# A new front half for a one-core decoder step: head in parts, rotation in place, four heads per score product, another job order

## The chip, the cores and the metric

One core of one Trainium2 chip runs the kernel. The metric is the device time of one execution in microseconds; lower is better.

## The reference, cut to what matters

One decoder layer over 256 prompt rows and 8 decode rows (264 columns in all, kept as features x rows), D = 1024, float32:

```
h = RMSNorm(x); proj = h @ w_in            # columns: pool u (512) | q (512) | k (512) | v (512)
mixer A: windows 2,4,8,16: trailing mean of u minus u, per-group map w_pool, scale s_pool
mixer B: attention, 8 heads x 64, rotary q and k; prompt rows causal over 256 keys,
         each decode row over its 256 paged keys (cache_k, cache_v) and its own key
x = x + concat(A, B) @ w_out
x = x + cross attention(RMSNorm(x)), 4 heads x 256, over 256 memory rows:
        prompt: mem_k, mem_v = RMSNorm(mem) @ w_ck, @ w_cv;  decode rows: cached memory keys and values
x = x + relu(RMSNorm(x) @ w_up)^2 @ w_down;  y = RMSNorm(x)
```

The outputs are y, the rotated k, v, the last rows of u, and the memory keys and values.

## The kernel before, in words

All weights stream through TensorE in 120 chunks of 256 rows x 512 columns (512 KB each). The groups stand in a fixed order: `in` 1 (q), `in` 2 (k), `in` 3 (v), `in` 0 (u), `ck`, `cv`, `out`, `cq`, `co` (chunks 0 to 55), then `up` and `down` (56 to 119). A product has to keep float32 precision with float32r operands, so each operand is split into a high part (ScalarE, line 881, `split_hi`, `w_hi<-raw`) and a low part (VectorE, line 1080, `split_lo`, `w_lo<-raw,w_hi`), and every tile is multiplied in three passes (high x high, high x low, low x high): 24 products of 264 columns a chunk at line 865. `raw` has 3 slots, `w_hi` and `w_lo` 4; a chunk is split three chunks ahead (`SPLITS_AT`), when the chunk four before it has been used.

The norm's factor is applied behind the product. ScalarE squares the tiles of x (`square`), GpSimd adds the squares (line 1306, `add_squares`), one product with ones sums over partitions (line 686, job `("stat", ...)`), ScalarE takes the root, VectorE the reciprocal (`rstd`).

The rest of the work is a list of jobs, each in a slot behind one chunk (`plan_jobs`); every engine walks through chunks and jobs in this one order. `S` h is the scores of prompt head h (lines 697 and 698, 64 rows of the array each, two products), followed on VectorE and ScalarE by mask, maximum, exponential and scaling; `P_T` transposes the probabilities (line 708), `O` multiplies by the values (lines 718, 719). `cS` b, `cP_T` b, `cO` b, `c_attn` b do the same for four decode rows each (b = 0, 1), on four column groups of 32 (helper `tile4`, line 666), with the products for the own key at lines 737 and 743; `c_attn` gathers the rows (line 753). `m_tile` k rounds a tile of the memory rows into `act_hi`/`act_lo`; `differences` and `pool` are mixer A; `xP_*` is the cross attention of the prompt, `xS`, `xc_T`, `xc_O`, `xc_attn` that of the decode rows (line 813 gathers).

The rotation of q and k (`take_out`, groups 1 and 2): ScalarE copies four quarters of a tile from PSUM with halves swapped (`swapped`), VectorE multiplies the tile by the cosines (line 1126), GpSimd the swapped one by the sines (line 1318), VectorE adds (line 1130). Group `in` 1 is in PSUM until `rstd` is there.

SyncE issues all loads in order: for each chunk first the units planned before it (`LOADS_AT`: pages of the caches `K`, `V`, memory rows `m`, memory keys `mK` and values `mV`, 512 KB each), then the weights (line 624). Four banks of PSUM belong to a running group; jobs take the bank that was used longest ago of the others.

Of the kernel before, what the change touches and what calls it, by code (L numbers as in the profile page):

```python
# [34 lines left out]
P = 128  # L35
# [24 lines left out]

CK = 2
# [3 lines left out]
AHEAD = SPLIT - 1  # L65
STAGE = 6
# [3 lines left out]
SOFTS = 3  # L70
SOFT_TS = 5
# [69 lines left out]
def plan_jobs():  # L141

    slots = {c: [] for c in range(-1, NC)}

    def put(c, *names):
        slots[c].extend(names)

    put(2, ("stat", "x"))
    k_end, v_end, u_end = last_chunk("in", 2), last_chunk("in", 3), last_chunk("in", 0)  # L160
# [3 lines left out]
    put(v_end + 1, ("v_nat", 0), ("v_nat", 1), ("v_nat", 2), ("cP_T", 0), ("m_tile", 0), ("m_tile", 1))  # L164
    put(v_end + 2, ("P_T", 2), ("P_T", 3), ("O", 0), ("m_tile", 2), ("m_tile", 3))
    put(v_end + 3, ("S", 4), ("S", 5), ("m_tile", 4), ("m_tile", 5))
    put(u_end, ("cO", 0), ("cS", 1), ("O", 1), ("m_tile", 6), ("m_tile", 7))
    put(u_end + 1, ("P_T", 4), ("P_T", 5), ("c_attn", 0))
    put(u_end + 2, ("cP_T", 1), ("S", 6), ("S", 7))
    put(u_end + 3, ("O", 2), ("stat", "m"), ("stat_col", "m"))  # L170
    put(u_end + 4, ("differences",))
    put(u_end + 5, ("P_T", 6), ("P_T", 7))
    put(u_end + 6, ("cO", 1), ("O", 3), ("pool", 0), ("pool", 1))
    put(u_end + 7, ("pool", 2), ("pool", 3), ("c_attn", 1))
    put(last_chunk("out", 1) + 3, ("stat", "c"))
    a, b = last_chunk("cq", 0), last_chunk("cq", 1)
# [12 lines left out]
ORDER = [j for c in range(-1, NC) for j in JOBS[c]]  # L189


def plan_banks():

    jobs, groups, uses, stamp, now = {}, {}, [0] * 8, [-1] * 8, 0
    hold_from, hold_to = ORDER.index(("xS", 0, 0)), ORDER.index(("xS", 1, 1))

    def take(bank):
        nonlocal now  # L200
        now += 1
        uses[bank] += 1
        stamp[bank] = now
        return uses[bank] - 1

    for c, (g, w, n, k, last) in enumerate(CHUNKS):
        if k == 0:
            for bank in banks_of(g):
                groups[g, bank] = take(bank)
        for j in JOBS[c]:  # L210
            if j[0] in ("m_tile", "differences"):
                continue
            if j[0] == "xS" and j != ("xS", 0, 0):
                jobs[j] = jobs["xS", 0, 0]
                continue
            taken = set(banks_of(g)) if not last else set() if (w, n) == ("cq", 1) or g + 1 == len(GROUPS) else set(banks_of(g + 1))
            if hold_from - 2 <= ORDER.index(j) <= hold_to:
                taken.add(7)
# [34 lines left out]


def plan_loads(kinds):

# [1133 lines left out]
```

## Time and profile before

| | us |
|---|---|
| median of 3 runs (lowest to highest) | 449.91 (447.57 to 452.04) |
| profiled execution: span from first to last instruction | 447.9 |
| TensorE busy | 423.8 |
| VectorE busy | 266.7 |
| ScalarE busy | 229.5 |
| GpSimd busy | 39.1 |
| moved by DMA | 96.8 MB, mean 216 GB/s |

The profile is of one execution, and its busy times are sums over its span of 447.9 us; its own time with what lies around the span is not recorded, so the span stands beside the median of the runs, 449.91. Matmuls are pipelined, so the distance between starts of two records says what one costs. A float32 product (no r) leaves two records.

### The profile page before, as it was taken

What the parts mean: (1) busy time and instruction counts of PE and PEld (TensorE: products, weight loads), DVE (VectorE), ACT (ScalarE), POOL (GpSimd) and SP (SyncE); (2) the same over time, 40 slices, a digit from 0 to 9 for tenths busy, and PEclk for the clock granted to TensorE, in tenths of its full rate; (3) what the DMA queues carried; (4) which work ended last, traced back from release to release, by engine and by line L of the source; (5) the groups of instructions that cost most, each with busy time, mean ns of one, the idle gap of its engine ahead of it and who ended that gap; (6) DMA issues with size and microseconds to landing.
All of it is one profiled execution on the core that took longest, in us unless ns stands there. A gap on an engine that the chain in (4) does not pass through costs nothing.

```text
span 447.9 us, 8424 instructions
## 1 busy us (share of the span) xinstructions
PE 423.8 (95%) x3346; PEld 393.0 (88%) x3346; DVE 266.7 (60%) x417; ACT 229.5 (51%) x411; POOL 39.1 (9%) x49
## 2 busy tenths in 40 slices
PE   2699899999999999999999999999999999999992
PEld 2699787787988999795599999999999999999992
DVE  2676787889454587654316967766666633444304
ACT  5777657664355474434026746656666533353202
POOL 0621001450000030000002200000000000020000
PEclk9979999999999999999989999999999999999998
DMA  7899897485699887597716655555555555545002
GB/s 273 286 280 343 324 265 240 161 283 170 185 352 317 334 277 284 173 368 281 266 36 246 235 190 187 189 190 189 187 187 184 186 180 176 176 168 179 1 1 97
DMA packets 42409, 96.80 MB, mean 216 GB/s; under 512 B 3954, under 2 KB 20466, under 8 KB 42234
## 3 DMA queue, kind: packets, MB, share of 16 engines
q1 hardware_dynamic: 40962, 93.03, 60.9%
q10 hardware_dynamic: 1408, 3.23, 1.9%
q8 instruction: 27, 0.44, 0.4%
q14 instruction: 12, 0.10, 0.1%
HBM read 91.94 MB, written 4.54 MB: 215 GB/s over the span
## 4 chain that ended last, share of the span: by engine, by line
PE 77%; ACT 8%; DVE 7%; issue 3%; DMA 2%; POOL 2%; ACTq 0%; SPq 0%; DVEq 0%; POOLq 0%
PE psum L865 68%; PE psum L666 4%; ACT w_hi L881 2%; DVE w_lo L1080 2%; DMA raw<-in_w_in 2%; POOL ssq L1306 1%; ACT swapped L881 1%; PE psum L791 1%; PE psum L778 1%; ACT soft L1024 1%; ACT act_hi L881 1%; DVE soft L1191 1%; PE psum L813 1%; DVE stats L1194 1%; PE psum L686 0%
## 5 line engine op out<-in xcount | busy, mean ns | idle before, releaser
L1080 DVE TENSOR_TENSOR w_lo<-raw,w_hi 128x1024 fp32r<-128x1024 f32 x82 | 103.1, 1268 | 90.5 <-ACT w_hi L881 90.0
L865 PE MATMUL psum<-act_hi,w_hi 128*128 128x264 f32 (+1 forms) x416 | 122.5, 294 | 9.0 <-DVE act_lo L1084 8.0
L881 ACT ACTIVATE w_hi<-raw 128x1024 fp32r<-128x1024 f32 x82 | 85.5, 1054 | 76.3 <-PE psum L865 64.2
L865 PE MATMUL psum<-act_lo,w_hi 128*128 128x264 f32 (+1 forms) x416 | 119.7, 288 | 0.0
L865 PE MATMUL psum<-act_hi,w_lo 128*128 128x264 f32 (+1 forms) x416 | 119.5, 287 | 0.0
L865 PEld LDWEIGHTS psum<-act_hi,w_hi 128*128 128x128 f32 x416 | 80.2, 193 | 12.9 <-DVE w_lo L1080 8.3
L865 PEld LDWEIGHTS psum<-act_lo,w_hi 128*128 128x128 f32 x416 | 80.0, 192 | 0.2
L865 PEld LDWEIGHTS psum<-act_hi,w_lo 128*128 128x128 f32 x416 | 79.8, 192 | 0.0
L1306 POOL TENSOR_TENSOR ssq<-ssq,sq 128x264 f32<-128x264 f32 (+1 forms) x31 | 25.4, 818 | 339.5 <-ACT sq L902 337.0
L865 PE MATMUL psum<-hid_hi,w_hi 128*128 128x264 f32 x176 | 50.1, 284 | 0.0
L865 PE MATMUL psum<-hid_lo,w_hi 128*128 128x264 f32 x176 | 50.1, 284 | 0.0
L865 PE MATMUL psum<-hid_hi,w_lo 128*128 128x264 f32 x176 | 50.0, 284 | 0.0
L865 PE MATMUL psum<-mix_hi,w_hi 128*128 128x264 f32 x128 | 37.2, 291 | 0.7 <-DVE mix_lo L1256 0.7
L865 PE MATMUL psum<-mix_hi,w_lo 128*128 128x264 f32 x128 | 37.2, 290 | 0.0
L865 PE MATMUL psum<-mix_lo,w_hi 128*128 128x264 f32 x128 | 37.1, 290 | 0.0
L865 PEld LDWEIGHTS psum<-hid_hi,w_hi 128*128 128x128 f32 x176 | 33.2, 189 | 0.0
L865 PEld LDWEIGHTS psum<-hid_lo,w_hi 128*128 128x128 f32 x176 | 33.1, 188 | 0.0
L865 PEld LDWEIGHTS psum<-hid_hi,w_lo 128*128 128x128 f32 x176 | 33.1, 188 | 0.0
L1080 DVE TENSOR_TENSOR w_lo<-raw_more,w_hi 128x1024 fp32r<-128x1024 f32 x16 | 19.5, 1231 | 15.3 <-ACT w_hi L881 15.3
L952 ACT ACTIVATE hid<-hid 128x264 f32<-128x264 f32 x32 | 13.3, 416 | 27.6 <-DVE hid L1146 27.6
L865 PE MATMUL psum<-act_lo,w_hi_more 128*128 128x264 f32 x96 | 27.3, 285 | 0.0
L865 PE MATMUL psum<-act_hi,w_hi_more 128*128 128x264 f32 x96 | 27.3, 284 | 0.0
(155 smaller groups left out, 769.1 us busy)
## 6 DMA issues: line engine op xcount, KB each, us to landing
raw<-in_w_down SPq DMA_DIRECT2D x20, 512.0 KB, 3.3
raw<-in_w_up SPq DMA_DIRECT2D x18, 512.0 KB, 4.3
raw<-in_w_in SPq DMA_DIRECT2D x16, 512.0 KB, 5.4
raw_more<-in_w_up SPq DMA_DIRECT2D x14, 512.0 KB, 4.4
raw_more<-in_w_down SPq DMA_DIRECT2D x12, 512.0 KB, 4.2
keysT<-in_cache_k SPq DMA_DIRECT2D x16, 256.0 KB, 4.4
stage<-in_cache_v SPq DMA_DIRECT2D x16, 256.0 KB, 4.1
raw<-in_w_ck SPq DMA_DIRECT2D x8, 512.0 KB, 5.2
```

What stands on the lines that cost most here:

```text
L666: return pe.matmul(out, lhsT, rhs, start=start, stop=stop, skip_group_check=True, tile_position=(0, 32 * j))
L778: last = pe.matmul(B[:, qt * MEM:(qt + 1) * MEM], q2T[:, 2 * h + d, qt * P:(qt + 1) * P], mkT[:, 2 * h + d, :], start=d == 0, stop=d == 1)
L791: last = pe.matmul(B[:, d * SEQ:(d + 1) * SEQ], mv[:, c, h * MHD + d * P:h * MHD + (d + 1) * P], pT[:, c * SEQ:(c + 1) * SEQ], start=c == ...
L813: last = pe.matmul(B[:, 4 * (AT * half + f):4 * (AT * half + f) + 4], opart[:, OPART["xc_O", b, half] % 2, f * P:(f + 1) * P], con("rowsel ...
L865: mm = pe.matmul(out, a, b, start=first and m == 0, stop=end_ and m == 2)
L881: return nc.scalar.activation(out, in_, ACT.Copy, scale=scale)
L952: nc.scalar.activation(hid[:, 1, j % 2, :], hid[:, 0, j % 2, :], ACT.Square).then_inc(square_ready, 1)
L1024: last = nc.scalar.activation(dst, src, ACT.Exp, bias=stats[:, slot, x:x + 1], accum_out=stats[:, slot, 2 + x:3 + x])
L1080: V.tensor_tensor(lo_of(c), raw_of(c), hi_of(c).bitcast(F32), ALU.subtract).then_inc(w_lo_ready, 1)
L1191: V.tensor_tensor(soft[:, slot, 0:3 * P], B[:, 0:3 * P], causal, ALU.add).then_inc(bank_free[PLACE[job][0]], 1)
L1194: V.tensor_reduce(stats[:, slot, 1:2], soft[:, slot, P:3 * P], AX_X, ALU.max, negate=True).then_inc(max_ready, 1)
L1306: nc.gpsimd.tensor_tensor(ssq[:, m % 2, 0:n], ssq[:, m % 2, 0:n], sq[:, k % SQ_SLOTS, 0:n], ALU.add).then_inc(sq_added, 1)
```

## The change

It leaves the weight products, their number and the second half (`up`, `down`) as they are, and rebuilds what stands before. In parts:

- **Head in parts.** The first weight tile is loaded, split and multiplied in two halves (`open_first_group`: pass by pass over four banks, not bank by bank). Gains and the first x tiles are issued by ScalarE. 16 products of zeros (`WARM`) run on TensorE first. `("stat", "x")` moves from slot 2 to slot 3.
- **Rotation in place.** The columns of `w_in` and of the key cache are ordered so that the two halves of a head lie in different tiles (`TURNED`). ScalarE copies each tile once to `qT` or `kT` and frees the bank; GpSimd makes two products with the sines a pair (`crossed`); VectorE turns the pair in place in the new jobs `("turn", 0)` (slot 4, with the tables) and `("turn", 1)` (slot 7).
- **Four heads per score product.** A head now has 32 rows in each of two tiles. `scores(four)` issues 16 products on four row groups of 32, into four banks. The softmax works on four heads (`exp` h on ScalarE, `norm` four on VectorE).
- **Decode rows of both halves in one bank.** `cS` 0 and 1 add up into one bank, with one softmax, one `cP_T`, one own-key product, one `c_attn`; the probabilities are spread with zeros (`own_q`, `rows_of`). For the cross attention `xS`, `xc_T`, `xc_O`, `xc_attn` go by half of the heads, with 8 rows at once.
- **Memory rows in the mixer's operand tiles.** `act_*` and `mix_*` change roles, so `m_tile` need not wait for the products of `in` 0.
- **New job order and loads.** Slots and `LOADS_AT` are written out; banks, those of the groups too, go to the one used longest ago.
- `pool_differences` works on four windows at once where it can.

```diff
-    put(2, ("stat", "x"))
-    put(k_end + 2, ("S", 0), ("S", 1))
-    put(k_end + 3, ("cS", 0))
-    put(v_end, ("P_T", 0), ("P_T", 1), ("S", 2), ("S", 3))
...
-    put(a + 1, ("xP_S", 0), ("xP_S", 1), ("xS", 0, 0))
-    put(a + 2, ("xS", 0, 1))
-    put(a + 3, ("xP_T", 0), ("xP_T", 1))
...
+    put(3, ("stat", "x"))
+    put(4, ("turn", 0))
+    put(7, ("turn", 1), ("m_tile", 0))
+    put(8, ("m_tile", 1))
+    put(9, ("k_out",), ("S", 0), ("S", 1), ("S", 2), ("S", 3), ("m_tile", 2))
+    put(10, ("exp", 0), ("exp", 1))
+    put(11, ("exp", 2), ("qblock",), ("exp", 3), ("norm", 0))
+    put(12, ("m_tile", 3))
+    put(14, ("P_T", 0), ("m_tile", 4), ("P_T", 1), ("P_T", 2), ("v_nat", 0))
+    put(15, ("m_tile", 5), ("P_T", 3), ("S", 4), ("S", 5), ("S", 6), ("S", 7), ("m_tile", 6), ("m_tile", 7), ("cS", 0))
+    put(17, ("exp", 4), ("stat", "m"), ("stat_col", "m"))
+    put(18, ("exp", 5))
+    put(19, ("exp", 6), ("differences",))
+    put(20, ("v_nat", 1), ("exp", 7))
+    put(21, ("v_nat", 2), ("norm", 1))
+    put(22, ("cS", 1))
+    put(23, ("O", 0), ("P_T", 4))
+    put(24, ("cP_T",), ("O", 1))
+    put(25, ("P_T", 5))
+    put(26, ("cO", 0))
+    put(27, ("P_T", 6))
+    put(28, ("pool", 0), ("P_T", 7))
+    put(29, ("pool", 1), ("cO", 1), ("pool", 2))
+    put(30, ("pool", 3), ("O", 2), ("O", 3))
+    put(32, ("c_attn",))
+    put(41, ("stat", "c"))
+    put(45, ("xS", 0, 0), ("xS", 0, 1), ("xP_S", 0), ("xP_S", 1), ("xc_T", 0))
+    put(46, ("xP_T", 0), ("xP_T", 1))
+    put(47, ("xc_O", 0, 0), ("xP_O", 0), ("xP_S", 2), ("xS", 1, 0), ("xS", 1, 1), ("xc_O", 0, 1), ("xP_O", 1), ("xc_attn", 0), ("xP_S", 3), ("xc_T", 1))
+    put(48, ("xP_T", 2), ("xc_O", 1, 0), ("xc_O", 1, 1), ("xP_T", 3))
+    put(49, ("xP_O", 2), ("xc_attn", 1), ("xP_O", 3))
...
+LOADS_AT = {
+    10: [("m", 0)],
+    14: [("m", 1)],
+    15: [("K", 0)],
...
+    22: [("K", 7), ("V", 0)],
+    23: [("K", 6), ("V", 1)],
+    24: [("K", 5), ("V", 2)],
+    25: [("K", 4), ("V", 3)],
...
+    52: [("mK", 1, 0), ("mK", 1, 1), ("mK", 1, 2), ("mK", 1, 3), ("mK", 1, 4), ("mK", 1, 5), ("mK", 1, 6), ("mK", 1, 7)],
+    54: [("mV", 1, 0, 2), ("mV", 1, 0, 3), ("mV", 0, 1, 0), ("mV", 0, 1, 1), ("mV", 0, 1, 2), ("mV", 0, 1, 3), ("mV", 1, 1, 0), ("mV", 1, 1, 1), ("mV", 1, 1, 2), ("mV", 1, 1, 3)],
+}
...
+            def scores(four):
+
+                if four == 0:
+                    pe.wait_ge(rope_done, PAIRS)
+                for j in range(4):
+                    begin(("S", 4 * four + j))
+                for out, queries, keys in ((0, 0, P), (P, P, SEQ)):
+                    for half in range(2):
+                        for j in range(4):
+                            r, f = 32 * j, 2 * four + half
...
+            def warm_up():
+
+                pe.wait_ge(warm_ready, 1)
+                for _ in range(WARM):
+                    pe.matmul(psum[:, 7, 0:P], std[:, 0:P], std[:, 0:P], start=True, stop=True)
...
+            def turn(g):
+
+                scale = HD ** -0.5 if g == group["in", 1] else 1.0
+                for i in range(2 * g, 2 * g + 2):
+                    x = 2 * (i % 2)
+                    pair = (qT if g == group["in", 1] else kT)[:, x:x + 2, :]
+                    dve.wait_ge(crossed_ready, i + 1)
+                    then(V.scalar_tensor_tensor(out=pair, in0=pair, scalar=scale, in1=turned[:, 0, :].unsqueeze(1).broadcast_to([P, 2, T]),
+                                                op0=ALU.mult, op1=ALU.mult))
```

## Rows read from the trace of the kernel before

**Rows 1.** The page: busy time by engine, and the chain's shares.
```profile
PE 423.8 (95%) x3346; PEld 393.0 (88%) x3346; DVE 266.7 (60%) x417; ACT 229.5 (51%) x411; POOL 39.1 (9%) x49
...
PE 77%; ACT 8%; DVE 7%; issue 3%; DMA 2%; POOL 2%; ACTq 0%; SPq 0%; DVEq 0%; POOLq 0%
```

**Rows 2.** Waits of TensorE: us in total, times, longest.
```profile
PE psum L865 <- DVE act_lo L1084: 8.0, 1, 8.0
PE psum L686 <- POOL ssq L1306: 4.1, 1, 4.1
PE psum L697 <- DVE kT L1130: 1.4, 1, 1.4
PE psum L865 <- DVE mix_lo L1256: 0.7, 1, 0.7
```

**Rows 3.** The chain that ended last: start, us, what.
```profile
259.90 177.84 PE psum L865 x1464
```

**Rows 4.** Timeline of TensorE, 8 to 23 us: start, duration, line.
```profile
8.03 0.56 PE L865 MATMUL psum<-act_hi,w_hi 128*128 128x264 f32 x1 [8.03 <-DVE act_lo L1084]
...
18.01 0.29 PE L865 MATMUL psum<-act_hi,w_lo 128*128 128x264 f32 x1
22.39 1.22 PE L686 MATMUL psum<-ssq,const 128*128 128x264 f32 x2 [4.10 <-POOL ssq L1306]
```

**Rows 5.** Chain and timeline of the first 23 us: transfers, ScalarE, GpSimd, SyncE.
```profile
3.08 7.71 DMA raw<-in_w_in
...
8.87 1.06 ACT L881 ACTIVATE w_hi<-raw 128x1024 fp32r<-128x1024 f32 x1 [2.31 <-DMA raw<-in_w_in]
...
17.85 2.04 SPq L601 DMA_DIRECT2D keysT<-in_cache_k  x2
...
18.05 4.19 POOL L1306 TENSOR_TENSOR ssq<-ssq,sq 128x264 f32<-128x264 f32 x4
```

**Rows 6.** Groups of instructions, 0 to 60 us: count, busy us, mean ns, idle before.
```profile
L881 ACT ACTIVATE swapped<-psum 32x264 f32<-32x264 f32 x32 | 12.2, 382 | 1.3 <-PE psum L865 0.8
...
L1318 POOL TENSOR_TENSOR rope_b<-swapped,turned 128x264 f32<-128x264 f32 x8 | 6.1, 768 | 18.3 <-ACT swapped L881 13.4 <-DVE turned L1121 4.9
```

**Rows 7.** Timeline of TensorE at its jobs, and one from the chain.
```profile
47.42 0.50 PE L697 MATMUL psum<-kT,qT 64*128 64x128 f32 x4 [1.35 <-DVE kT L1130]
47.71 0.64 PE L698 MATMUL psum<-kT,qT 64*128 64x256 f32 x4
...
57.04 0.48 PE L697 MATMUL psum<-kT,qT 64*128 64x128 f32 x2
57.37 0.59 PE L698 MATMUL psum<-kT,qT 64*128 64x256 f32 x2
...
76.13 1.12 PE L743 MATMUL psum<-v_nat,ownp 8*128 8x512 f32 x2
...
86.14 0.95 PE L753 MATMUL psum<-const,opart 128*128 128x4 f32 x8
...
89.88 0.38 PE L735 MATMUL psum<-const,soft 128*128 128x128 f32 x2
...
179.14 3.45 PE psum L778 x16
...
182.52 1.94 PE L666 MATMUL psum<-keysT,qblock 128*32 128x256 f32 x32
...
222.91 1.95 PE L813 MATMUL psum<-const,opart 128*128 128x4 f32 x16
```

**Rows 8.** Windows: us, busy time by engine, granted clock, DMA share, GB/s.
```profile
24.00:28.00 4.00, 4.00 (x20) 4.00 (x19) 3.40 (x6) 3.07 (x9) 0.75 (x1) 0.50 0.87 254
...
84.00:224.00 140.00, 139.10 (x1052) 117.24 (x1052) 86.69 (x152) 64.22 (x116) 14.07 (x13) 1.00 0.77 268
...
188.00:200.00 12.00, 12.00 (x102) 10.80 (x95) 5.38 (x8) 4.57 (x7) 0.00 (x0) 1.00 1.04 350
...
224.00:228.00 4.00, 3.29 (x20) 3.23 (x20) 0.19 (x1) 0.20 (x1) 0.00 (x0) 0.74 0.00 0
```

More of the change, by code:

```diff
@@ L58 @@
 NKEY = PAST + 1
+PAIRS = AT
 CK = 2
@@ L167, in plan_jobs @@
[L167 to L175, printed above, removed]
@@ L189 @@
 ORDER = [j for c in range(-1, NC) for j in JOBS[c]]
+CHUNK_OF = {j: c for c in JOBS for j in JOBS[c]}
+CLOSER = {("cS", 0): ("cS", 1), ("cO", 0): ("cO", 1)}
+CLOSER |= {(what, half, 0): (what, half, 1) for what in ("xS", "xc_O") for half in range(2)}
+OPENER = {closer: opener for opener, closer in CLOSER.items()}
+NO_PRODUCTS = ("m_tile", "differences", "turn", "qblock", "k_out", "exp", "norm", "split")
 def plan_banks():
-    jobs, groups, uses, stamp, now = {}, {}, [0] * 8, [-1] * 8, 0
-    hold_from, hold_to = ORDER.index(("xS", 0, 0)), ORDER.index(("xS", 1, 1))
@@ L199, in take, with touch, oldest @@
-    def take(bank):
+    jobs, groups, banks, uses, held, now = {}, {}, [], [0] * 8, set(), 0
+    stamp = list(range(-8, 0))
+    def touch(bank):
         nonlocal now
         now += 1
+        stamp[bank] = now
+    def take(bank):
+        touch(bank)
         uses[bank] += 1
-        stamp[bank] = now
         return uses[bank] - 1
+    def oldest(n, taken):
+        return sorted(set(range(8)) - taken - held, key=lambda b: stamp[b])[:n]
     for c, (g, w, n, k, last) in enumerate(CHUNKS):
@@ L215, in plan_banks @@
                 continue
-            taken = set(banks_of(g)) if not last else set() if (w, n) == ("cq", 1) or g + 1 == len(GROUPS) else set(banks_of(g + 1))
-            if hold_from - 2 <= ORDER.index(j) <= hold_to:
-                taken.add(7)
-            bank = 7 if j[0] == "xS" else min(set(range(8)) - taken, key=lambda b: stamp[b])
+            if j[0] == "S":
+                if j[1] % 4 == 0:
+                    four = oldest(4, set() if last else set(banks[g]))
+                jobs[j] = (four[j[1] % 4], take(four[j[1] % 4]))
+                continue
@@ L220, in plan_banks, with banks_of @@
+            [bank] = oldest(1, set() if last else set(banks[g]))
+            if j in CLOSER:
+                held.add(bank)
             jobs[j] = (bank, take(bank))
-    return jobs, groups
-PLACE, GROUP_PLACE = plan_banks()
+    return jobs, groups, banks
+PLACE, GROUP_PLACE, GROUP_BANKS = plan_banks()
+def banks_of(g):
+    return GROUP_BANKS[g]
 def turns(kinds):
@@ L1059, in _ @@
                     take_out(c)
-                if not halfway(c):
-                    for s in SPLITS_AT.get(c + 1, ()):
-                        split_hi(s)
+                if not halfway(c) and ("split",) not in JOBS[c]:
+                    split_next(c)
                 for job in JOBS[c]:
-                    run(job)
+                    if job == ("split",):
+                        split_next(c)
+                    else:
+                        run(job)
         @block.vector
```

618 lines of the change are left out of this document (363 added, 255 removed).

## The prediction

> **What bounds the kernel now.** I read the page first. TensorE is busy 95% of the span and carries most of the chain [rows 1], so I asked where it is not busy and what it does that could be less. Its waits come next: one of 8.0 us before the first product, one of 4.1 us for the square sums of `("stat", "x")`, one of 1.4 us before the first scores, and five more of 0.7 us down to 0.2, 2.3 us in all [rows 2]. All the rest of the 447.9 us is products standing back to back, except 10 us behind the last weight product. A weight chunk (24 products of 264 columns) takes 24 x 177.84/1464 = 2.92 us [rows 3]. No transfer and no other engine holds TensorE after the head. So the change is worth what it takes off TensorE's own list, off the head, and off those waits. The third view is the granted clock. Between 18.0 and 22.4 TensorE idles, and from 23 to 28 the records start 0.22 us apart and not 0.12; the 4 us window from 24 shows clock 0.50, which is 1.2 GHz, while 2.4 GHz is granted around it [rows 4, 8]. It falls once more at the end of the cross attention: 0.74 in the window from 224, after the four-column products `L813` and the 0.7 us wait [rows 2, 7, 8].
>
> **The head.** Before, chunks 0 to 2 end at 18.3, the statistic comes at 22.39 and chunk 3 ends near 28.1 [rows 4]. After:
> - The first weight half tile and x go out 0.5 us earlier, on two queues, and 16 products warm the engine. Chunk 0 is then done by 8.5 to 10.4 instead of 12.3 (12 products at 0.22, 12 at 0.12). But chunk 1 needs the second weight tile, and TensorE is held by transfers here: the third weight tile took 7.71 us to land, until 10.8 [rows 5]. The second was waited for until 8.87 [rows 5]. Half a microsecond earlier, plus rounding (1.0), two roundings of x (0.8) and low halves (1.1 and 0.9, partly beside them) gives chunk 1 at 11.5, so chunk 2 ends near 17.4. Only 0.9 us of the 4 is kept.
> - The warm-up: 8 float32 products of 256 columns took 3.45 us at full clock [rows 7], so 128 columns take 0.22, at half clock 0.43. 16 of them are 6.9 us if nothing rises, from about 1 us on. It lies wholly in the 8.0 us wait, so I book it at nothing; without that cover it would cost up to 2.
> - `("stat", "x")` moves behind chunk 3, whose end is 20.3. The square sums are seven additions at about 0.9 us apart [rows 5], with the first now near 13, so they end at 19.5 and the 4.1 us wait is gone. The statistic ends at 20.65 against 23.0, and chunk 3 stands ahead of it. Chunk 3 also ran at half clock before, (0.22 - 0.12) x 21 = 2.1 us. End of chunk 3 and statistic: 28.1 - 20.65 = 7.5 us earlier.
> The Trainium skill says that DMAs issued from several engines run on the same DMA engines and that this only saves issue time ("Trainium Kernel Development and Optimization", Key Constraints). By that rule the second queue gives 0.5 us and not a faster landing, which is what the 0.9 us above comes to; nobody who leaves this out changes a number.
>
> **The rotation.** ScalarE's 32 swapped quarter copies (12.2 us busy) become 8 plain ones (3 us), GpSimd keeps 8 multiplications of 0.77 [rows 6], VectorE keeps as much. But TensorE now comes earlier than the rest of the chain. With chunk 9 ending at 20.65 + 6 x 2.92 = 38.1, `turn(1)` must wait for `turn(0)` (statistic, reciprocal 1.8, tables 0.8, two pairs at 1.55 on GpSimd, in order with the splits on VectorE), for the raw tiles in ScalarE's queue, and for two more pairs. With tiles that land 4 us after their issue the walk is: statistic's root 25.5 (behind tile 7 in ScalarE's queue), reciprocal 27.3, split of chunk 8 and tables 29.2, pairs crossed 30.5 and 32.0, `turn(0)` done 33.6, three splits to 37.0, two pairs of `turn(1)` 40.0. With 3.3 us to land it ends at 39.3, with 5.4 (the median of the `w_in` tiles on the page) at 41.4. I take 40.0: a wait of 1.9 us, so the first scores start 47.4 - 40.0 = 7.4 us earlier; bounds 6.0 and 8.1. Queued behind a waiting `turn` on VectorE are the `w_lo` splits, each three chunks ahead of use.
>
> **TensorE's own list, before against after.**
> - Scores: a pair of heads standing back to back takes 0.86 us (47.42 to 48.28), but heads 2 and 3 did not overlap and took 2.01 [rows 7]; the other two pairs took 0.86. Sum 4.59. After: two blocks of 8 products of 128 and 8 of 256 columns, on four row groups at once. The nearest row is 16 products of 256 columns on four column groups, 1.9 us [rows 7], 0.117 each; half of them 128 wide gives 1.42 a block, 2.84 in all: -1.75 us. The other end is no overlap, with the prices of heads 2 and 3 (0.33 and 0.6 us a product): 2 x 8 x 0.93 = 14.9 us, +10. I take the near end, because those pairs show two row groups running together.
> - `cP_T` once instead of twice (0.31 + 0.31): -0.6. The own-key product `L743` once: -1.05. `c_attn` once: -0.8. `xc_attn`: 8 products instead of 16; each four-column product costs 0.24 by its weight load, not by its columns, so half of 2 x 1.95: -1.95 [rows 7]. Sum -4.4.
> - Waits: the 0.7, 0.6, 0.5, 0.3 and 0.2 go (2.3 us), as every consumer stands one chunk or more behind its producer. New ones: `cS` 1 opens only once `("P_T", 4)` is done, a chunk later; VectorE stands there for 4 us with `take_out(23)` and the split of chunk 27 behind it, both with a chunk to spare. The last memory values `mV` can only go out after `("xS", 1, 0)` and queue behind ten other units. At 350 GB/s, the rate of the window 188 to 200 [rows 8], a unit of 0.52 MB takes 1.5 us, and the last four land about 2 us after `("xc_O", 1, 1)` could start. I book 1.5. Net -0.8.
> - Clock: the fall at 226 costs 1.7 us. It followed the thin products and a wait. These are halved and dense chunks stand between them, but a new wait of 1 to 2 us is close. I book half: -0.9.
> - Three more places where jobs cut into the chunks, at 0.13 us: +0.4.
> Memory rows in the other operand tiles, the LRU banks and the softmax over four heads take nothing off TensorE. They shorten VectorE's list, which is not late. The cover is the three chunks (9 us) by which splits lead.
>
> The Trainium skill adds a rule against this change: "Mode switching requires drain" ("TensorEngine Tiling (Array Packing)", Key Properties). By it each block of scores pays a drain on entry and exit; the pairs of before switched modes as well, four times against two now, so the sum would if anything gain some tenths. The page "TensorE: Matmul & The Clock Gate" (Measured speedup vs the span model) has 3.07 times for four row groups; by that the blocks would take 1.7 us each, 0.5 us more in all.
>
> **The sum** for the profiled execution: 7.4 + 1.75 + 4.4 + 0.8 + 0.9 - 0.4 = 14.9 us, so a span of 433.0 against 447.9. The span stands 2.0 us under the median of the runs, 449.9, and I carry that distance: **435.0 us**.
>
> **Rivals.**
> - *The head gives little.* The rotation chain ends later still, or the clock falls in the gap between chunks 0 and 1 and chunks 1 and 2 run at 1.2 GHz (+3). For it: that gap is 1 to 3 us, and one of 4.1 us did drop the clock [rows 2, 8]. Against: the wait of 1.4 us did not. Gain 8 to 9 in all: 441. Chance 0.13.
> - *The four score products don't overlap.* Heads 2 and 3 show that queued pairs may run one after the other. Then +10 instead of -1.75: 447, or 441 if half of it overlaps. Chance 0.08, half of it above 445.
> - *The waits go to the in-order queues.* From the load at 22 on, SyncE issues two page transfers for each of eight K and V units at 1.0 us each [rows 5], behind the end of `cS` 0, some 4.4 us a chunk against 2.9 on TensorE. ScalarE stands for the raw tile of chunk 25, and with it the copies of `v_nat` and `P_T`. My slack is 2 to 3 us there, 1 us for the values before `("cO", 1)`. If it is used up: 440 to 443. Chance 0.08.
> - *Slower than before: the transfers bind.* Between job slot 15 and the last `xc_O` the kernel must move 33 weight chunks, 44 units and 2.6 MB of outputs, 42.7 MB in about 143 us, or 298 GB/s. The same stretch of before moved 268 GB/s on average [rows 8]. If that were the limit, it would take 159 us and the whole gain is lost; below 262 GB/s the kernel is over 1% slower. Against: 350 GB/s over 12 us with TensorE going on. Time 455. Chance 0.03.
> - *More than forecast.* The clock stays up, no new wait appears, and gaps in the timeline that no wait names go too (the second half of `("O", 1)` took 0.97 us where others take 0.32). 429. Chance 0.12.
>
> **Chances and range.** The forecast, 431 to 439, has 0.56. The range of 428 to 444 leaves out the upper half of the scores case, the slower case and the far end of the good one. A measurement of this kernel tells about 1% from no change. Faster by over 1% means under 445.4: all but the serial scores (0.04), the transfers (0.03) and a small part of the queues. I give 0.92, within 1% 0.05, slower 0.03.
>
> **What would show it.** Right: `("stat", "x")` without a wait longer than 0.5 us and a full clock from about 6 us on; first scores at 39 to 41.5; a block of scores at 1.4 to 1.7 us; `L743` and `cP_T` once; the second half from the statistic of `c` on unchanged at 2.92 us a chunk. Wrong: a wait of TensorE on `w_lo` or `raw` anywhere between chunks 4 and 60, a clock of 0.5 in the stretch from 10 to 20, score blocks over 3 us, or an `xc_O` that stands for `stage` over 3 us.

## The result, and the profile after

The changed kernel takes 438.7 us (median of 4 runs, 437.8 to 439.5); the kernel before took 448.9 beside it (4 runs, 447.6 to 452.0). The ratio is 0.976, 95% interval 0.972 to 0.980: faster by 2.4%. The profiled execution has a span of 436.2 us against 447.9, so 11.7 us less. Forecast were 435.0 us and 14.9 us less.

In the medians the gain is 10.2 us (448.9 - 438.7). The kernel before was 1.0 us faster beside the changed one than the 449.9 that I had started from, and the distance from the profiled span to the median is 2.5 us after, where I carried 2.0.

The page of the changed kernel, in the two lines that answer to [rows 1]:

```profile
PE 419.4 (96%) x3380; PEld 390.9 (90%) x3380; DVE 262.1 (60%) x370; ACT 221.0 (51%) x386; POOL 43.1 (10%) x52
...
PE 72%; DVE 9%; DMA 7%; issue 4%; SPq 4%; ACT 3%; POOL 0%; ACTq 0%; DVEq 0%; POOLq 0%
```

TensorE is still busy for nearly all of the span. The waits of TensorE answer to [rows 2]:

```profile
PE psum L753 <- DVE kT L1308: 3.4, 1, 3.4
PE psum L753 <- DVE uext L1263: 1.6, 1, 1.6
PE psum L924 <- POOL std L1490: 1.0, 1, 1.0
PE psum L779 <- POOL ssq L1487: 0.7, 1, 0.7
PE psum L974 <- DVE w_lo L1221: 0.7, 1, 0.7
PE psum L793 <- DVE soft L1385: 0.6, 1, 0.6
PE psum L740 <- DMA keysT<-in_mem_v: 0.2, 1, 0.2
```

The 8.0 us at the start are filled with warming products (`L924`), and the 4.1 us at the first square sums are 0.7. Of the two score blocks (`L753`) the first waits 3.4 us for the rotated keys, where the old kernel waited 1.4, and the second 1.6 us for `uext`, where it waited for nothing. The timeline of TensorE says where (start, duration, line, idle before), with the jobs that the change halves, for comparison with [rows 7]:

```profile
20.62 0.68 PE L779 MATMUL psum<-ssq,const 128*128 128x264 f32 x2 [0.71 <-POOL ssq L1487]
20.94 0.48 PE L974 MATMUL psum<-act_hi,w_hi 128*128 128x264 f32 x1
...
43.23 1.59 PE L753 MATMUL psum<-kT,qT 32*128 32x128 f32 x32 [3.43 <-DVE kT L1308]
44.75 0.39 PE L974 MATMUL psum<-act_hi,w_hi 128*128 128x264 f32 x1
...
66.15 1.59 PE L753 MATMUL psum<-kT,qT 32*128 32x128 f32 x32 [1.63 <-DVE uext L1263]
...
109.30 1.12 PE L828 MATMUL psum<-v_nat,ownp 8*128 8x512 f32 x2
...
135.31 0.95 PE L837 MATMUL psum<-const,opart 128*128 128x8 f32 x8
...
218.25 0.95 PE L891 MATMUL psum<-const,opart 128*128 128x8 f32 x8
```

A block of scores takes 44.75 - 43.23 = 1.52 us. The own-key product and `c_attn` stand once; `xc_attn` (`L891`) is two jobs of four products (eight records), 0.81 us each up to the start of the next product, where [rows 7] has one of two jobs of 1.95. Chain and windows answer to [rows 3, 8]:

```profile
247.72 178.30 PE psum L974 x1464
```

```profile
32.00:36.00 4.00, 3.88 (x33) 3.67 (x31) 3.97 (x6) 3.20 (x8) 2.54 (x4) 1.00 0.04 13
...
44.00:48.00 4.00, 4.00 (x42) 3.66 (x35) 4.00 (x6) 1.23 (x7) 0.80 (x1) 1.00 1.06 368
...
84.00:224.00 140.00, 139.10 (x1071) 114.55 (x1070) 75.70 (x128) 62.33 (x112) 5.94 (x8) 1.00 0.82 299
224.00:228.00 4.00, 4.00 (x35) 4.00 (x34) 2.34 (x4) 2.05 (x4) 0.00 (x0) 1.00 0.14 23
```

The second half is unchanged: its chain of 1464 products takes 178.30 us, against 177.84. The clock never falls before the tail. What I hadn't looked for stands in the first window: between 32 and 36 us the transfers move 13 GB/s, against 329 in the same window of before, and from 44 on they run at 368.

Three marks on TensorE carry the comparison, since the work ahead of each is the same in all kernels with the new job order: start of the first scores, start of the memory's statistic (`("stat", "m")`, behind the second score block), and end of the last weight product. They read 43.23, 75.89 and 425.83; before, the first and the last were at 47.42 and 437.56. The stretch from the second mark to the third is not quite constant. It takes between 349.6 and 351.6 us, longest in the run with the sines on VectorE. Part of the difference is TensorE's wait for probabilities at `("P_T", 4)`, near 97 us: 0.6 us in the changed kernel, 1.2 with the sines on VectorE, 1.5 with all three edits. The rest I did not trace. So a gain at the second mark need not reach the third in full.

### The profile page after: what moved, and what is told of

The parts are those of the page before. It is cut to its first block, busy times and chain, and to the rows that moved or that the text cites. A ratio compares the mean times of both kernels' runs of the same rounds, so it can differ in the third digit from the quotient of the medians.

```text
span 436.2 us, 8397 instructions
## 1 busy us (share of the span) xinstructions
PE 419.4 (96%) x3380; PEld 390.9 (90%) x3380; DVE 262.1 (60%) x370; ACT 221.0 (51%) x386; POOL 43.1 (10%) x52
## 4 chain that ended last, share of the span: by engine, by line
PE 72%; DVE 9%; DMA 7%; issue 4%; SPq 4%; ACT 3%; POOL 0%; ACTq 0%; DVEq 0%; POOLq 0%
PE psum L974 63%; DVE w_lo L1221 4%; PE psum L740 4%; DMA raw<-in_w_in 2%; DMA keysT<-in_mem_v 2%; DMA raw<-in_w_cv 1%; DMA raw<-in_w_ck 1%; PE psum L871 1%; PE psum L858 1%; SPq L666 1%; SPq L644 1%; ACT w_hi L990 1%; DVE act_lo L1225 1%; DVE mix_lo L1225 1%; SPq L691 1%
## 5 line engine op out<-in xcount | busy, mean ns | idle before, releaser
L990 ACT ACTIVATE w_hi<-raw 128x1024 fp32r<-128x1024 f32 (+1 forms) x83 | 86.1, 1045 | 80.0 <-PE psum L974 49.6
L974 PE MATMUL psum<-mix_hi,w_hi 128*128 128x264 f32 (+1 forms) x288 | 82.9, 288 | 0.2 <-ACT softT L990 0.2
L974 PE MATMUL psum<-mix_lo,w_hi 128*128 128x264 f32 (+1 forms) x288 | 81.6, 283 | 0.0
L974 PE MATMUL psum<-mix_hi,w_lo 128*128 128x264 f32 (+1 forms) x288 | 81.6, 283 | 0.0
L974 PE MATMUL psum<-act_hi,w_hi 128*128 128x264 f32 x248 | 71.5, 288 | 0.9 <-DVE w_lo L1221 0.7
L974 PE MATMUL psum<-act_hi,w_lo 128*128 128x264 f32 x248 | 70.5, 284 | 0.0
L974 PE MATMUL psum<-act_lo,w_hi 128*128 128x264 f32 x248 | 70.4, 284 | 0.0
L974 PEld LDWEIGHTS psum<-mix_hi,w_hi 128*128 128x128 f32 x288 | 54.3, 189 | 1.4 <-issue 0.8
L974 PEld LDWEIGHTS psum<-mix_lo,w_hi 128*128 128x128 f32 x288 | 54.3, 188 | 0.1
L974 PEld LDWEIGHTS psum<-mix_hi,w_lo 128*128 128x128 f32 x288 | 54.1, 188 | 0.0
L1221 DVE TENSOR_TENSOR w_lo<-raw_more,w_hi 128x1024 fp32r<-128x1024 f32 x16 | 19.5, 1230 | 15.2 <-ACT w_hi L990 15.2
```

Source lines behind the costliest of these rows:

```text
L974: mm = pe.matmul(out, a, b, start=first and m == 0, stop=end_ and m == 2)
L990: return nc.scalar.activation(out, in_, ACT.Copy, scale=scale)
L1221: V.tensor_tensor(lo_of(c), raw_of(c), hi_of(c).bitcast(F32), ALU.subtract).then_inc(w_lo_ready, 1)
```

## The experiments

Times are medians of 4 to 10 runs, with the lowest and highest; ratios are to the kernel before on the same chip. One profile each. The kernels were measured on several chips, so two of them are compared by their ratios, and a difference of half a per cent between two ratios lies within their intervals.

| kernel | us | ratio, 95% interval | first scores | statistic m | last product |
|---|---|---|---|---|---|
| changed | 438.7 (437.8–439.5) | 0.976 (0.972–0.980) | 43.23 | 75.89 | 425.83 |
| split behind the turn | 438.7 (438.5–439.0) | 0.972 (0.967–0.978) | 41.26 | 75.92 | 426.79 |
| sines on VectorE | 437.8 (437.0–438.4) | 0.970 (0.965–0.975) | 41.70 | 73.62 | 425.20 |
| GpSimd kept busy | 439.8 (one) | | 45.26 | 77.90 | 427.64 |
| memory scores first | 438.7 (436.8–439.0) | 0.971 (0.966–0.977) | 43.55 | 76.33 | 426.50 |
| no warming | 437.6 (436.4–438.3) | 0.973 (0.967–0.979) | 43.37 | 75.12 | 424.70 |
| statistic in slot 2 | 439.6 (439.0–442.1) | 0.979 (0.973–0.985) | 45.69 | 77.53 | 427.26 |
| three edits | 439.2 (437.7–440.2) | 0.976 (0.971–0.981) | 40.65 | 75.22 | 426.39 |
| before, warmed | 449.2 (447.5–452.3) | 0.999 (0.996–1.002) | 46.12 | | 435.36 |
| pages early | 437.0 (435.2–437.9) | 0.971 (0.967–0.975) | 43.28 | 75.16 | 425.41 |
| three edits, three pages | 437.6 (435.8–439.6) | 0.973 (0.969–0.978) | 40.03 | 73.72 | 423.87 |
| three edits, two pages | 435.7 (434.5–436.1) | 0.968 (0.964–0.972) | 40.39 | 71.86 | 422.54 |
| the same, no warming | 435.5 (434.6–436.4) | 0.968 (0.964–0.972) | 41.45 | 73.03 | 423.11 |

### Why the first scores came at 43.2 and not at 40.0

VectorE and GpSimd from the first turn on, in the changed kernel (timelines; start, duration):

```profile
30.54 1.16 DVE L1305 SCALAR_TENSOR_TENSOR qT<-qT,turned 128x528 f32<-128x528 f32 x1 [1.44 <-POOL crossed L1505]
31.74 0.88 DVE L1307 SCALAR_TENSOR_TENSOR qT<-crossed,qT 128x264 f32<-128x264 f32 x1
32.53 0.42 DVE L1308 SCALAR_TENSOR_TENSOR qT<-crossed,qT 128x264 f32<-128x264 f32 x1
...
35.31 4.59 DVE L1221 TENSOR_TENSOR w_lo<-raw,w_hi 128x1024 fp32r<-128x1024 f32 x3
39.83 0.69 DVE L1305 SCALAR_TENSOR_TENSOR kT<-kT,turned 128x528 f32<-128x528 f32 x1
```

```profile
30.39 0.76 POOL L1504 TENSOR_TENSOR crossed<-qT,turned 128x264 f32<-128x264 f32 x1
31.10 1.23 POOL L1505 TENSOR_TENSOR crossed<-qT,turned 128x264 f32<-128x264 f32 x1
...
35.65 1.48 POOL L1504 TENSOR_TENSOR crossed<-kT,turned 128x264 f32<-128x264 f32 x1 [0.55 <-ACT kT L990]
37.09 1.73 POOL L1505 TENSOR_TENSOR crossed<-kT,turned 128x264 f32<-128x264 f32 x1
```

The same operation takes 0.42 us in one row and 0.88 in another, and GpSimd's product 0.76 and 1.73. The long ones lie beside a long one of the other engine. Three splits end 4.52 us after they began, 1.5 each instead of 1.14. Two theories: the engines hold each other up (A), or the last split in front of `turn(1)` is all that is late (B).

**Split behind the turn.** Slot 7 names the split of chunk 11, so that VectorE does it after the keys. (Some of the expectations below call it chunk 10.)

```diff
-    put(7, ("turn", 1), ("m_tile", 0))
+    put(7, ("turn", 1), ("split",), ("m_tile", 0))
```

> The changed kernel with the split of chunk 11 moved behind the second half of the rotation (slot 7). Theory A (VectorE's list, slowed while GpSimd works, sets the first scores): turn 1 starts when two splits instead of three are done, 38.3 instead of 39.8, so the first scores start at 41.7 instead of 43.2 and the span is 1.5 us shorter, 434.7. Theory B (late weight tiles in ScalarE's queue set it): kT copies come 1.4 us earlier, but GpSimd still ends near 38 and the span moves by under 0.5 us.

**Sines on VectorE.** GpSimd's eight products go to VectorE.

```diff
-                    dve.wait_ge(crossed_ready, i + 1)
...
+                    V.tensor_tensor(crossed[:, i % 2, 0, :], tile[:, x + 1, :], turned[:, 1, :], ALU.mult)
+                    then(V.tensor_tensor(crossed[:, i % 2, 1, :], tile[:, x, :], turned[:, 1, :], ALU.mult))
```

> The changed kernel with the eight sine products of the rotation on VectorE instead of GpSimd. Theory A (GpSimd and VectorE slow each other): a pair takes 2 x 0.36 + 0.63 + 2 x 0.36 = 2.1 us with nothing beside it, turn 0 ends at 33.3 instead of 35.4, the three splits take 3.4 instead of 4.5 us, turn 1 ends at 41.1; first scores at 41.2 instead of 43.2, span 434.2. Theory B (late tiles, or simply VectorE's list): VectorE has 2.9 us more to do, first scores at 43.2 to 46, span 436 to 439.

**GpSimd kept busy.** Behind its last sine product GpSimd adds a tile that nobody needs yet, eight times.

```diff
...
+            for i in range(8):
+                gp.wait_ge(extra_pool, i + 1)
+                nc.gpsimd.tensor_tensor(sums[:, 0, 0, 0:T], sums[:, 0, 0, 0:T], sums[:, 0, 0, 0:T], ALU.add).then_inc(extra_pool, 1)
```

> The changed kernel with eight more additions of 128x264 on GpSimd, on a tile nobody reads yet, behind its last sine product (38.8 to 46 us). Theory A: the six instructions of turn 1 take 0.9 to 1.2 and 0.8 us instead of 0.65 and 0.35, the first scores start 1.5 to 2 us later, near 45. Theory B: nothing on the way to the scores has become longer, first scores stay at 43.2 within 0.3.

VectorE with the sines on it, then GpSimd and VectorE in the run with GpSimd kept busy (timelines):

```profile
29.47 0.71 DVE L1309 SCALAR_TENSOR_TENSOR qT<-qT,turned 128x528 f32<-128x528 f32 x1
...
33.14 3.49 DVE L1221 TENSOR_TENSOR w_lo<-raw,w_hi 128x1024 fp32r<-128x1024 f32 x3
```

```profile
39.27 7.19 POOL L1511 TENSOR_TENSOR sums<-sums 128x264 f32<-128x264 f32 x8
```

```profile
39.93 1.13 DVE L1306 SCALAR_TENSOR_TENSOR kT<-kT,turned 128x528 f32<-128x528 f32 x1
```

Three splits are 3.41 us again and the wide operation 0.71, so although VectorE has eight operations more, the first scores start 1.5 us sooner (41.70 against 43.23). Extra work on GpSimd that nothing on the way to the scores waits for makes them 2.0 us later (45.26). On the slowing both speak for A, though the spans that A had named did not come: 436.6 against 434.2 with the sines on VectorE, and 437.2 against 434.7 with the split behind the turn. The next section has a reason for the second. The split behind the turn also gives 2.0 us (41.26): it was in the way, but a split at 1.14 would have been less so. In the changed kernel the slowing is 1.9 us in `turn(0)` (30.54 to 35.31 for two pairs, against 2 x 1.43 in the run with the sines on VectorE, its products apart), 1.1 in the splits (4.52 - 3.41) and 0.4 in `turn(1)`: 3.4 us, which covers the miss of 3.2. Transfers are not behind it: from 32 to 36 us, where the operations are long, they move 13 GB/s in the changed kernel and none in the one with the split behind the turn.

The Trainium skill has this ("SBUF — State Buffer", SBUF: two separate sides): GpSimd and a VectorE operation with two inputs in SBUF share a pair of ports, which is "an **exclusive lock**, not a bandwidth split", so that the later one stands until the earlier has ended. The rows agree in direction, but the slowing is smaller than a lock held for whole instructions would give. With GpSimd kept busy VectorE's two pairs of `turn(1)` take 5.19 us (39.93 to 45.12) against 2 x 1.43 alone, and in that time GpSimd does five whole additions of at least 0.69 us each: 6.3 us of work in 5.2. (GpSimd's records are the rougher ones.) The rows also fit the rows that I had priced from: in the kernel before, VectorE's `rope_a` reads one input from PSUM, and its product of 0.43 us from 32.97 beside GpSimd's 0.76 from 32.96 slowed neither.

### Why 2 us sooner there were worth nothing

The split behind the turn started the scores 2.0 us sooner. TensorE at its two score blocks (timeline):

```profile
41.26 0.39 PE L753 MATMUL psum<-kT,qT 32*128 32x128 f32 x4 [1.89 <-DVE kT L1308]
...
66.19 0.39 PE L753 MATMUL psum<-kT,qT 32*128 32x128 f32 x4 [1.64 <-DVE uext L1263]
```

The second block starts at 66.19, in the changed kernel at 66.15. Between them TensorE waited 0.56 and 1.25 us for probabilities and their copies.

**Memory scores first.** `cS` 0, which waits for neither `uext` nor the banks that VectorE is emptying, goes ahead of the second block.

```diff
-    put(15, ("m_tile", 5), ("P_T", 3), ("S", 4), ("S", 5), ("S", 6), ("S", 7), ("m_tile", 6), ("m_tile", 7), ("cS", 0))
+    put(15, ("m_tile", 5), ("P_T", 3), ("cS", 0), ("S", 4), ("S", 5), ("S", 6), ("S", 7), ("m_tile", 6), ("m_tile", 7))
```

> The changed kernel with the scores against the paged keys (cS 0) ahead of the second block of prompt scores in slot 15. If the wait of 1.6 us there is for the four banks of group in 0, which VectorE is still emptying, the 1.9 us of cS 0 cover it: wait under 0.2, span 1.4 to 1.6 us shorter (434.7). If it is the pages' landing or the softmax that is late, the wait only moves to cS 0 or to P_T 4 and the span stays at 436.

The wait at the block is gone, yet the last product comes 0.7 us later. The first scores of this execution, and the window behind them:

```profile
43.55 0.60 PE L753 MATMUL psum<-kT,qT 32*128 32x128 f32 x4 [3.56 <-DVE kT L1308]
```

```profile
44.00:48.00 4.00, 4.00 (x39) 3.20 (x36) 4.00 (x6) 1.24 (x7) 0.72 (x1) 0.50 1.07 372
```

The granted clock is 0.50 there, 1.2 GHz, against 1.00 in the changed kernel's own window. The clock's records give 6.8 us at that level, 3.4 us of work. So the edit's gain and a fall of the clock can't be told apart in one profile, and the median (438.7) shows no gain.

**All three edits.** The split, the sines and the memory scores together.

> The changed kernel with three edits: sine products on VectorE, the split of chunk 11 behind turn 1, cS 0 ahead of the second block of scores. Theory A: turn 0 ends at 33.3, two splits 35.6, turn 1 39.8; first scores at 40.0 with a wait of 2 us, too short to halve the clock; no wait in slot 15; span 431.5 to 433, ratio to before 0.965. Theory B (what is gained at the scores is given back by the next late tile, as with the split behind alone): first scores at 40 but the statistic of m and all behind it within 1 us of the changed kernel, span 435 to 436.

The scores start at 40.65, near the 40.0 forecast for the change itself. At the memory's statistic only 0.7 of 2.6 us are left, and the last product comes 0.6 us later than in the changed kernel (426.39), in a span of 437.7. That is worse than B had named (435 to 436). Five waits stand between the first two marks, 3.5 us in all, on VectorE's `soft` and `uext` and ScalarE's `softT`. Behind all of them is ScalarE (the timeline of this kernel):

```profile
58.42 1.06 ACT L990 ACTIVATE w_hi<-raw 128x1024 fp32r<-128x1024 f32 x1 [2.91 <-DMA raw<-in_w_ck]
```

ScalarE stands for a weight tile, and for the next one 2.35 us more, with the copies of the transposed probabilities behind it in its queue. The changed kernel has the same two waits, 2.76 and 1.90 us. Why the tile is late, SyncE's queue says (changed kernel):

```profile
25.50 3.27 SPq L691 DMA_DIRECT2D raw<-in_w_in  x2
...
36.56 2.01 SPq L691 DMA_DIRECT2D raw<-in_w_in  x2
...
39.94 0.33 SPq L691 DMA_DIRECT2D raw<-in_w_in  x1
41.29 2.01 SPq L666 DMA_DIRECT2D keysT<-in_cache_k  x2
...
48.80 1.36 SPq L691 DMA_DIRECT2D raw<-in_w_ck  x1
```

From 28.8 to 36.6 SyncE issues nothing: the next weight load waits for a raw tile that VectorE, busy with the turns, hasn't split. This is the hole of 13 GB/s. The key pages need no tile of that ring, but stand behind the load in the list, and then share the transfers with the weights.

The split moved behind the turn makes this worse, and I had not seen it. The load of chunk 14 needs the tile that the split of chunk 11 frees. SyncE issues it at 39.94 in the changed kernel and at 42.90 with the split behind the turn. The same load with the sines on VectorE alone, then with all three edits (two timelines), and the second score block with the sines alone:

```profile
36.66 0.33 SPq L691 DMA_DIRECT2D raw<-in_w_in  x1
```

```profile
41.75 0.33 SPq L691 DMA_DIRECT2D raw<-in_w_in  x1
```

```profile
64.27 1.59 PE L753 MATMUL psum<-kT,qT 32*128 32x128 f32 x32
```

With the sines alone ScalarE does not wait for `w_ck` ahead of the second block (its first such wait is at 79.45), and that block has no wait in front. The memory's statistic is at 73.62, 1.6 us ahead of the three edits, although the first scores start 1.05 us later and 1.7 us go to the clock. So part of what the three edits give back probably comes from the edit of the split. The memory scores first differ between the two runs as well, and nothing separates them. No run has the sines on VectorE with the pages early and the split where it was.

**Pages early.** The only edit is to `LOADS_AT` of the changed kernel.

```diff
-    14: [("m", 1)],
-    15: [("K", 0)],
-    16: [("K", 1)],
-    17: [("K", 2)],
-    18: [("K", 3)],
+    12: [("K", 0), ("K", 1), ("K", 2)],
+    14: [("m", 1)],
+    16: [("K", 3)],
```

> The changed kernel with one edit of SyncE's list: the key pages of samples 0 to 2 are asked for ahead of weight chunk 12, that of sample 3 ahead of chunk 16, instead of one sample each ahead of chunks 15 to 18. In the changed kernel the transfers move 13 GB/s from 32 to 36 us, because SyncE stands at a weight load whose tile VectorE has not freed, and 252 to 368 GB/s from 44 to 64 us, where the pages go beside one weight chunk in 2.9 us; ScalarE then waits 2.76 and 1.90 us for w_ck. Theory A (the pages beside the weights make w_ck late, and with it the transposes and the second score block): the six page loads go in the hole from 29 to 36 us, ScalarE's two waits for w_ck shrink below 1 us, the second score block starts without its wait of 1.63 us (at 64.5 instead of 66.15 when the first scores start at 43.2), and the last weight product ends at 424.2 instead of 425.8: 437.1 us. Theory B (the vector engines' own work sets the second block): ScalarE waits less but TensorE still waits 1.3 to 1.6 us there, 438.7. Theory C (SyncE issues pages when the tiles come free, and chunks 12 and 13 come later): a new wait of 0.5 to 2 us ahead of the first scores, 439 to 441. The wait at the first scores stays at 3.4 in A and B; a clock fall behind it would add 1.7 to 3.4 us to each.

Windows of this kernel, and its second score block:

```profile
32.00:36.00 4.00, 4.00 (x36) 4.00 (x34) 3.93 (x7) 3.33 (x8) 2.75 (x3) 1.00 0.76 206
44.00:48.00 4.00, 4.00 (x31) 3.63 (x27) 4.00 (x6) 2.40 (x8) 2.91 (x2) 0.59 1.00 371
```

```profile
65.78 0.39 PE L751 MATMUL psum<-kT,qT 32*128 32x128 f32 x4
```

The hole is filled, ScalarE's waits for the landing of `w_ck` ahead of the block are gone, and the block has no wait in front, although the first scores are where they were. The start of the block is only 0.4 us sooner; this execution lost 1.7 us to the clock (0.59 in the second window). Now ScalarE waits for chunk 12 instead, 6.82 us against 3.64. The median is 437.0 against 438.7, the ratio 0.971 against 0.976 with overlapping intervals: the mechanism is shown in the trace, a gain in time is likely and not proven by this pair.

**Three edits and three pages early.** The same list under the three edits.

> The kernel with the three edits (split of chunk 10 behind the second turn, crossed products on VectorE, memory scores ahead of the second score block) and the key pages of samples 0 to 2 ahead of weight chunk 12 as well. With the three edits alone the first scores started at 40.65 (2.6 us ahead of the changed kernel) but TensorE then waited 0.64, 1.10, 0.53, 0.64 and 0.62 us between 57 and 71 us, while ScalarE waited 2.91 and 2.35 us for w_ck, and the statistics of the memory started at 75.22 against 75.89: 2.0 of 2.6 us given back. Theory A (late pages and weights are what takes the gain back): ScalarE's waits for w_ck go below 1 us, TensorE's five waits fall from 3.5 us to under 1.5, the statistics start at 73.2, the whole takes 436.0 to 437.0 us. Theory B (VectorE, busy 3.9 of each 4 us up to 60 us, takes it back, since it now does the crossed products as well): the waits stay above 2.5 us and the time at 438.5 to 439.5.

```profile
43.00 1.06 ACT L988 ACTIVATE w_hi<-raw 128x1024 fp32r<-128x1024 f32 x1 [8.40 <-DMA raw<-in_w_in]
```

```profile
59.55 0.30 PE L791 MATMUL psum<-const,soft 128*128 128x128 f32 x1 [2.55 <-DVE soft L1387]
```

`w_ck` isn't late any more, as A says, but now a weight chunk of `in` is, and the probabilities with it: TensorE waits 2.9 us in all behind the first scores, up to the statistic of the memory, as B says. The time, 437.6, lies between the two. The late tile is chunk 12, asked for at 36.59. (The next expectation calls it chunk 13, which was split right behind it, at 44.67.) Whether the pages delayed it or VectorE is the bound, the next kernel asks.

**Three edits and two pages early**, with samples 2 and 3 ahead of chunks 16 and 17.

```diff
-    12: [("K", 0), ("K", 1), ("K", 2)],
+    12: [("K", 0), ("K", 1)],
     14: [("m", 1)],
-    16: [("K", 3)],
+    16: [("K", 2)],
+    17: [("K", 3)],
```

> The kernel with the three edits (split of chunk 10 behind the second turn, crossed products on VectorE, memory scores ahead of the second score block) and with the key pages of two samples, not three, ahead of weight chunk 12; samples 2 and 3 ahead of chunks 16 and 17. With three samples there the waits for w_ck were gone, but ScalarE waited 8.40 us for weight chunk 13 (it began to split it at 43.00, asked for at about 37.1), VectorE 2.59 us behind it, and TensorE 2.55 us for the probabilities at 59.55. Theory A (pages ahead of a weight chunk and pages beside w_ck are the same cost in two places, and two samples fit in the hole of 29 to 35 us): chunk 13 is split by 41.5, TensorE's wait at the probabilities is under 1.2 us, the second score block ends by 66.5, the last weight product at 422.5 instead of 423.9: 436.0 us. Theory B (VectorE, which now holds the crossed products too, is what is late): chunk 13 comes earlier but the wait for the probabilities stays over 2 us and the time at 437.6. A clock fall behind the first scores, as in some kernels with a wait of 3 us there, isn't expected (the wait is 1.6 to 2.0).

```profile
57.73 0.30 PE L792 MATMUL psum<-const,soft 128*128 128x128 f32 x1 [0.92 <-DVE soft L1388]
...
64.39 0.39 PE L752 MATMUL psum<-kT,qT 32*128 32x128 f32 x4
```

```profile
244.42 178.30 PE psum L973 x1464
```

All of theory A's marks hold: wait 0.92 (under 1.2), block ended at 65.9 (66.5), last product 422.54 (422.5), 435.7 us (436.0); chunks 12 and 13 are split at 39.82 and 41.49. That some agree to the tenth is partly luck, since the last stretch varies by up to 2 us between kernels. VectorE with the same work was no obstacle. All six runs (434.5 to 436.1) lie below all runs of the changed kernel, and the ratios, 0.968 (0.964 to 0.972) against 0.976 (0.972 to 0.980), just part: about 0.8% faster.

### The head

**No warming.** Two runs: `WARM` set to 0 in the changed kernel, and in the version with three edits and two pages early.

> The changed kernel without the 16 warming products. Theory A (the head is held by transfers, the warm-up only saves the half clock of chunks 0 and 1): TensorE starts near 5.2 us at half clock, chunk 0 is done before 9, chunk 1 still starts at 10 to 11 and perhaps one or two us of it run at 0.22 us a product, so the statistic stands at 20.5 to 22 and the span is 0 to 1.5 us longer. Theory B (the warm-up is what keeps the clock up through the gap before chunk 1): the clock is 0.5 to about 14 or later, the statistic comes 3 to 4 us later and the span is 439 to 440.

> The same kernel without the warming products. Theory A (the first statistics set the head: without warming, chunk 0 went at half clock and the statistics still ended at 20.9): the same as with them, within 1 us. Theory B (warming is what keeps the clock up at the first scores: of the kernels with it and a wait of 3 us or more there, three had the clock fall and one did not, of those without it one of one): the clock falls for 3.4 or 6.8 us at 43, 1.7 to 3.4 us longer.

Without warming, in the changed kernel, chunk 0 starts at 6.13, its records 0.22 us apart, and chunk 1 at 11.55 instead of 10.92. The statistic is at 20.61 as with it. With warming TensorE waits there for the square sums, which end at 20.47; without it TensorE arrives just then, so the 0.6 us come out of the waits of 0.2 and 0.7. The times are the same within what a run can tell, both times. The warming products buy nothing here.

**Statistic in slot 2** (`STAT_X` = 2 in the changed kernel), as it stood before.

> The changed kernel with the statistic of x back behind chunk 2 instead of chunk 3. Theory A (moving it is what gives the head its gain): TensorE waits at 17.3 for the square sums until 20.5, over 3 us, chunk 3 and the statistic end 3 us later than 20.9, or 5 to 6 later where the wait also halves the clock. But the first scores are set by VectorE's list from the statistic on, which comes at the same 20.6: they start at 43 to 44 all the same, so of the 3 to 6 us only 0 to 2 reach the end: span 436 to 438. Theory B (the head's gain reaches the end in full): span 439 to 442.

```profile
20.14 0.68 PE L779 MATMUL psum<-ssq,const 128*128 128x264 f32 x2 [3.86 <-POOL ssq L1487]
```

The wait is back, the clock falls behind it, and the first scores come 2.5 us later, at 45.69, which neither theory had (A said 43 to 44). Of these, 1.4 reach the last product: 0.9 us in the median, with ratios whose intervals overlap (0.973 to 0.985 against 0.972 to 0.980), so the direction is shown in the trace and not in the times. By its code the kernel before can't have this step alone (no run tries it): there VectorE takes out chunk 3's group only with the reciprocal, which it would make only after that.

**Before, warmed.** The kernel before with 16 warming products.

> The kernel before with 16 warming products on TensorE and nothing else. They run from 1 to at most 8 us, inside its wait of 8.0 us. Theory A (transfers hold chunk 1): chunk 0 gains 1.2 us, chunk 1 starts within 0.5 us of where it did, the wait for the statistic grows by what was gained (4.1 to 4.5 or more) and the halved clock behind it stays: span 447.5 to 448. Theory B: the span falls by 1.2 us or more.

Two windows of this kernel:

```profile
22.00:26.00 4.00, 4.00 (x21) 3.94 (x21) 3.90 (x4) 3.05 (x9) 0.00 (x0) 0.61 0.81 248
224.00:228.00 4.00, 3.28 (x27) 3.23 (x27) 0.19 (x1) 0.20 (x1) 0.00 (x0) 1.00 0.00 0
```

The wait of 4.2 us still drops the clock, and 449.2 us is no gain. But the fall at 226 of [rows 8] isn't there, with the same thin products and the same wait in front. So the fall at 226 comes in some executions of the old work and not in others.

## Why the prediction was right, and where it was off

The time was in the range and on the right side; the sum was 3.2 us too large, and all of that lies ahead of the first scores.

- **Head, -7.5.** Right within 0.3: the statistic's end, forecast for 20.65, is at 20.94. Warming at nothing was right, shown twice. Chunk 1 begins at 10.9, forecast for 11.5. Two errors nearly cancel: the square sums start at 12.0, not 13, but I had read them 0.9 us apart where [rows 5] has 4.19 us for four, and here five take 6.08. They end at 20.47, not 19.5, and the wait of 0.7 is over the 0.5 that I had allowed.
- **Rotation walk: the term that was mis-sized.** Forecast for the first scores 40.0, bounds 39.3 to 41.4; measured 43.23. The walk held up to its first turn (30.5 forecast, 30.54 measured). Then "`turn(0)` done 33.6, three splits to 37.0, two pairs of `turn(1)` 40.0" became 35.3, 39.8 and 43.2. I had priced each engine alone, from [rows 6] and from splits at 1.14 us, out of a kernel in which VectorE and GpSimd mostly took turns by data or had an operand in PSUM. Here both read SBUF from 30.5 to 38.8 with short gaps. One of my signs of being wrong came with it: TensorE waits 0.7 us on `w_lo` at 36.58, in chunk 9. It cost nothing, since the wait for the keys behind it would have taken it in.
- **From the first scores to the last weight product** the forecast was 1.75 + 4.4 + 0.8 + 0.9 - 0.4 = 7.45 us; the traces give 390.1 - 382.6 = 7.5. The total is right by luck, since errors of about a microsecond cancel:
  - Scores 1.52 and 1.53 a block against 1.42: -1.5 instead of -1.75. The rival of serial products fell. (The 1.7 by the Trainium skill's 3.07 times, quoted in the prediction, was too long by 0.2 a block.)
  - Jobs halved: own key 1.05, `c_attn` 0.8 and `cP_T` 0.6 as forecast, `xc_attn` from 3.9 to 1.6, -2.3 against -1.95.
  - Waits: forecast -0.8, measured +0.3 (2.6 us in four waits, where 2.3 stood before). The new one at `xc_O(1,1)` is 0.2, not 1.5, but 1.6 us stand at the second score block and 0.6 at the probabilities, where I had expected none. "Every consumer stands one chunk or more behind its producer" failed there.
  - Clock: -1.7 us in this pair of executions, against -0.9 booked. After the warmed run I can't credit this to the change.
- **In-order queues (0.08).** I had this rival at slots 22 to 25. The mechanism is real, but it stands at slots 15 to 18, behind a hole of 8 us in SyncE's list. I looked at what the loads pass late, not at what an engine that gets busier (VectorE at the turns) does to a list that waits for it. What the first scores at 40.0 would have brought in the changed kernel stays open: the three edits keep 0.7 us of 2.6 at the statistic of the memory, but one of them itself delays a weight load.
- **Transfers bind (0.03).** Over 84 to 224 us they moved 299 GB/s, the rate that I had worked out as needed, with 0.2 us of wait: no.

## What to carry to other kernels

Price an operation that is moved beside another engine's work from a row in which both run, not from one in which they take turns. When one engine's list gets longer in one place, look which ring of tiles it frees, and what stands in an in-order queue behind the load that waits for it: loads that need nothing of the ring belong ahead of that one, as many as the hole holds and no more. When an earlier start changes nothing two jobs later, look for the mark that didn't move (here 66.15 and 66.19), follow its wait to its root, and ask whether the edit itself made something else late.

## What the runs showed that I had not expected

VectorE and GpSimd slowed each other where both read SBUF: VectorE's 128x264 operation 0.43 to 0.88 us, GpSimd's product 0.75 to 1.73, a split 1.14 to 1.5 on average. TensorE's clock fell to 1.2 GHz behind a wait of 2.9 to 3.6 us at the first scores in five profiled kernels (sines on VectorE, memory scores first, no warming, statistic in slot 2, pages early), and behind 5.4 us in the one with GpSimd kept busy, but not in the changed kernel with 3.43; behind 1.6 to 2.0 us it never fell. Each fall cost 1.7 or 3.4 us. In the version with two pages early the wait is 1.7 us, and its runs show a mean clock of 0.993 to 0.995, against 0.988 to 0.993 of the changed kernel, so part of its gain is probably that it keeps away from that point. The span ended 2.9 us after the last operation of any engine in the changed kernel and 3.9 us after it in the version with two pages early, whose tail does the same work. That distance is 3.8 to 3.9 us in all five kernels with the sines on VectorE and 2.8 to 2.9 in all the others, so about 1 us of what they gain is lost there; why stays open.
